# Where the moving tiles of a 256-token transformer kernel lie relative to its weight tiles, modulo 512 bytes

## The reference

```
for layer in range(2):                            # first block, N = 256 tokens
    h = h + mixer(rmsnorm(h, g))                  # x @ w_in, ..., @ w_out
    a, b = split(rmsnorm(h, g2) @ w_in)           # 1024 -> 2 x 3072
    h = h + (gelu(causal_dwconv(a)) * b) @ w_out  # 3072 -> 1024
for l in range(2):                                # second block: 512 tokens (x and context), then 256
    branches, gates = split_in(modulate(rmsnorm(x)) @ w_in[l])
    x = x + g1 * (sum(sigmoid(gate) * (branch @ w_branch)) @ w_out[l])
    x = x + g2 * swiglu(modulate(rmsnorm(x)), w_ffn_in[l], w_ffn_out[l])
return rmsnorm(x, final_g)
```

## Time and profile before

| | us |
|---|---|
| median of 3 runs | 2056.38 |
| lowest and highest run | 2051.12, 2064.75 |
| the profiled execution's own time | 2058.86 |
| its span in the trace | 2057.1 |
| TensorE busy | 1981.9 (96%) |
| VectorE busy | 1498.4 (73%) |
| ScalarE busy | 897.0 (44%) |
| GpSimd busy | 361.3 (18%) |
| TensorE instructions | 12926 matmuls, as many weight loads |

### The profile page before, as it was taken

The page is one execution under the profiler, slowest core; times in us unless marked ns, Lnnn a source line. Parts: engine busy times, 40 slices in busy tenths (PEclk is TensorE's granted clock), DMA queues, the critical chain, the costliest instruction groups (busy, mean ns, idle before and its releaser), DMA issues.

```text
span 2057.1 us, 33908 instructions
## 1 busy us (share of the span) xinstructions
PE 1981.9 (96%) x12926; PEld 1751.6 (85%) x12926; DVE 1498.4 (73%) x2820; ACT 897.0 (44%) x1436; POOL 361.3 (18%) x354
## 2 busy tenths in 40 slices
PE   6999999989999999989999999999999998998998
PEld 6999999859999988646888878888888866998998
DVE  7769987687987698776687667575666986675554
ACT  5744444473445532575343332222224356654443
POOL 0013233002325400001100312202231000013223
PEclk9999999899999999999999999999999999999999
DMA  6455575505555432103345325454563311554552
GB/s 261 164 195 194 190 262 180 198 11 216 201 183 210 166 110 82 42 1 116 131 183 179 117 83 205 143 202 166 204 216 142 141 45 43 184 188 161 188 201 83
DMA packets 46991, 318.15 MB, mean 155 GB/s; under 512 B 5008, under 2 KB 8080, under 8 KB 9488
## 3 DMA queue, kind: packets, MB, share of 16 engines
q1 hardware_dynamic: 45568, 309.60, 41.8%
q0 software_dynamic: 1296, 6.82, 1.0%
HBM read 315.34 MB, written 1.05 MB: 154 GB/s over the span
## 4 chain that ended last, share of the span: by engine, by line
PE 88%; DVE 5%; ACT 4%; issue 1%; POOL 1%; DMA 0%; DVEq 0%; POOLq 0%; ACTq 0%
PE ps L674 85%; ACT arena L1249 3%; PE ps L959 2%; DVE arena L2092 2%; DVE w_lo L1664 1%; ACT w_hi L1249 1%; DVE small L1896 0%; POOL arena L574 0%; DVE arena L1918 0%; PE ps L1152 0%; DMA x<-x_in 0%; POOL arena L570 0%; DVE arena L1646 0%; ACT L1249 0%; PE ps L1145 0%
## 5 line engine op out<-in xcount | busy, mean ns | idle before, releaser
L674 PE MATMUL ps<-h_hi,w_hi 128*128 128x256 f32 (+2 forms) x2656 | 841.0, 317 | 18.0 <-DVE h_lo L1656 6.3
L674 PE MATMUL ps<-h_lo,w_hi 128*128 128x256 f32 (+2 forms) x2656 | 833.4, 314 | 0.0
L674 PE MATMUL ps<-h_hi,w_lo 128*128 128x256 f32 (+2 forms) x2656 | 833.0, 314 | 0.0
L1664 DVE TENSOR_TENSOR w_lo<-ring,w_hi 128x1024 fp32r<-128x1024 f32 x457 | 584.8, 1286 | 291.9 <-ACT w_hi L1249 291.1
L1249 ACT ACTIVATE w_hi<-ring 128x1024 fp32r<-128x1024 f32 x457 | 479.7, 1056 | 516.6 <-PE ps L674 482.8
L674 PEld LDWEIGHTS ps<-h_hi,w_hi 128*128 128x128 f32 (+1 forms) x2656 | 504.4, 190 | 55.6 <-issue 12.2
L674 PEld LDWEIGHTS ps<-h_lo,w_hi 128*128 128x128 f32 (+1 forms) x2656 | 503.3, 189 | 32.3
L674 PEld LDWEIGHTS ps<-h_hi,w_lo 128*128 128x128 f32 (+1 forms) x2656 | 502.7, 189 | 32.4
L1249 ACT ACTIVATE arena<-ps 128x512 f32<-128x512 f32 (+2 forms) x246 | 141.2, 580 | 341.3 <-PE ps L674 297.0
L674 PE MATMUL ps<-hid_hi,w_lo 128*128 128x256 f32 (+1 forms) x736 | 224.0, 304 | 0.0
L674 PE MATMUL ps<-hid_hi,w_hi 128*128 128x256 f32 (+1 forms) x736 | 224.0, 304 | 0.0
(11 more groups left out here) (195 smaller groups left out, 1945.3 us busy)
## 6 DMA issues: line engine op xcount, KB each, us to landing
ring<-wstream SPq DMA_DIRECT2D x290, 1024.0 KB, 4.8
arena<-c_in POOLq DMA_DIRECT2D x7, 512.0 KB, 4.0
arena<-rpb POOLq DMA_DIRECT2D x2, 1536.0 KB, 7.0
x<-x_in SPq DMA_DIRECT2D x2, 1024.0 KB, 12.3
out<-arena SPq DMA_DIRECT2D x8, 128.0 KB, 2.0
cst<-consts SPq DMA_DIRECT2D x1, 940.0 KB, 12.2
prm<-params SPq DMA_DIRECT2D x1, 580.0 KB, 10.9
ring<-wstream SPq DMA_DIRECT2D x1, 512.0 KB, 3.9
```

The lines of the kernel that those rows point to most:

```text
L674: ins = nc.tensor.matmul(*a, **k)
L1664: V.tensor_tensor(w_lo[:, job % SPLITS, :], raw_job(job), w_hi[:, job % SPLITS, :].bitcast(F32), ALU.subtract).then_inc(weights_ready, 1)
```

## The change

It changes the byte offsets of operands and nothing else. The view `h_at[S]` starts 32 floats in, where it started 48 in. The spacer is 16 floats shorter, which moves the arena, and hid_hi and hid_lo behind it, down by 64 bytes. The padding below branch_hi is 16 floats longer, so branch_hi keeps its address, and its view for 256 columns starts 32 floats in. The view of hid_hi and hid_lo for 512 columns starts 32 floats in, where it started 16 in, so it keeps its address as well.

```diff
--- before.py
+++ after.py
@@ -313,7 +313,7 @@
         w_lo = sb("w_lo", [P, SPLITS, JOB * P], F32R)
         x = sb("x", [P, KD, S2])
         h_rows = [sb(n, [P, KD * S2 + 128], F32R) for n in ("h_hi", "h_lo")]
-        h_at = {n: [v[:, at:at + KD * S2].rearrange("p (k t) -> p k t", t=S2) for v in h_rows] for n, at in ((S, 48), (S2, 0))}
+        h_at = {n: [v[:, at:at + KD * S2].rearrange("p (k t) -> p k t", t=S2) for v in h_rows] for n, at in ((S, 32), (S2, 0))}
         prm = sb("prm", [P, PARAM["end"]])
         cst = sb("cst", [P, CONST["end"]])
         ones = sb("ones", [P, P])
@@ -324,7 +324,7 @@
         mod_parts = sb("mod_parts", [P, 48, 2, 2])
         gn = sb("gn", [P, 2, 2, KD])
 
-        sb("spacer", [P, 128 - KD - HEADS])
+        sb("spacer", [P, 112 - KD - HEADS])
         with nc.sbuf_tensor("arena", [P, ARENA], F32) as arena:
             pass
         with ExitStack() as over:
@@ -336,9 +336,9 @@
             cy_lo = place("cy_lo", KC * S2)
             place("below_naq", 4096, F32)
             naq_lo, gq_lo = place("naq_lo", KC * S2), place("gq_lo", KC * S2)
-            place("below_hi", 17104 - 15616, F32)
-            hi_rows = place("branch_hi", 48 + KC * S2)
-        branch_hi = {n: hi_rows[:, at:at + KC * S2].rearrange("p (c t) -> p c t", t=S2) for n, at in ((S, 48), (S2, 0))}
+            place("below_hi", 17120 - 15616, F32)
+            hi_rows = place("branch_hi", 32 + KC * S2)
+        branch_hi = {n: hi_rows[:, at:at + KC * S2].rearrange("p (c t) -> p c t", t=S2) for n, at in ((S, 32), (S2, 0))}
         branch_lo = [v[:].rearrange("p (c t) -> p c t", t=S2) for v in (naq_lo, gq_lo, cy_lo)]
         hid_hi = sb("hid_hi", [P, KF1 * S + 128], F32R)
         hid_lo = sb("hid_lo", [P, KF1 * S + 128], F32R)
@@ -369,7 +369,7 @@
         m_silu, m_prod = (part(hidden_end + i * 2 * S2, 2, S2) for i in range(2))
         f_out = part(0, KD, S)
         f_hidden = [v[:, 0:KF1 * S].rearrange("p (c t) -> p c t", t=S) for v in (hid_hi, hid_lo)]
-        m_hidden = {n: [v[:, at:at + KF1 * S].rearrange("p (c t) -> p c t", t=S2) for v in (hid_hi, hid_lo)] for n, at in ((S, 0), (S2, 16))}
+        m_hidden = {n: [v[:, at:at + KF1 * S].rearrange("p (c t) -> p c t", t=S2) for v in (hid_hi, hid_lo)] for n, at in ((S, 0), (S2, 32))}
 
         n_q = part(0, KD, S)
         n_kc = part(2048, 2, KV, S)
```

## The result

| | before | after |
|---|---|---|
| median, us | 2057.82 | 2082.81 |
| lowest and highest of 6 runs, us | 2051.12, 2066.25 | 2081.76, 2086.03 |
| ratio, with 95% interval | | 1.0121 (1.0095 to 1.0147) |
| span of the profiled execution, us | 2057.1 | 2083.9 |

The forecast was 2049 us in a range of 2036 to 2066; the time lies outside, on the side of rival (d). The page of the kernel after has the same shape as the earlier trace rows: TensorE busy for 96%, the clock at 90% or more in every slice, L674 with 85% of the chain. TensorE's busy time grew by 27.9 us (1981.9 to 2009.8) and the span by 26.8, so what was lost is TensorE's own time; VectorE's busy time stayed (1498.4 to 1498.2).

A forecast was written before the change was run, and what follows sets the result against it. TensorE was taken as the bound: its instruction count times their pace. The profiled 2058.9 us less 9.7 for the quick pace everywhere, small terms at 0, gave 2049.2, said as 2049 us; range 2036 to 2066.

The forecast's parts named there:

- rival (d): 256-column matmuls moved to 128: always the middle pace, 22.6 us more, 2081 us; chance 0.06.
- the count of slow matmuls: 256-column products in the kernel before: 2211 matmuls said to run at a slow pace, taking 258.4 us.
- the seven stretches: Parts of the kernel before at the slow pace, 258.4 us; the quick pace there would save 9.7 us.
- The upper bound of the unknown pace: 256-column matmuls at 128: at most the 120.0 ns seen at 0, which would cost 39.5 us more.
- the reading of the scatter: Runs of the kernel before: may differ by which stages are slow; one feed-forward layer changing pace is 6.6 us.
- a single pace at 128: 256-column matmuls after the change: one pace only, so the after runs would lie close together.
- I take the quick pace, 113.3: 256-column matmuls at 128: 113.3 ns chosen within the bounds, 9.7 us less than the profiled execution.
- reached 113.3 in 7 of 10 matmuls: 256-column matmuls at 192, the nearest row to 128: mostly 113.3 ns, used as ground for 113.3 at 128.
- (c): 256-column matmuls: pace repeats every 128 bytes, so 128 is like 0, 120.0 ns each, 2098 us; chance 0.12.
- (b): 256-column matmuls at 128: conflict vanishes wholly, only the weight load is left, 2036.7 us or 2035; chance 0.08.
- floor of 111.6 ns: Weight load in every matmul, read from matmuls with 60 moving columns; 12.5 us below the quick pace over 7344 matmuls.
- (a): 256-column matmuls at 128: same two paces as 192, 113.3 and 117.7 ns, 2056 us (2050 to 2063); chance 0.16.

The follow-up runs named there:

- bare loop: Kernel before without the reference's computation, TensorE alone running product triples at many operand offsets: 113.3 ns at 192, 120.0 at 0, 118.8 at 128 behind plain matmuls.

## Why the prediction was wrong

**Right.** TensorE's pace at L674 is what sets the time and what the change changes; nothing else in the program moved. The paces, the addresses (0 modulo 256 for the 120.0, 192 for the two of before), and the count of slow matmuls are borne out: the sum over the quick pace, 11.6 us in the kernel before, has the 9.7 us of the seven stretches in it. The upper bound of the unknown pace was right: 118.7 and 120.0 lie in 113.3 to 120.0. So was the reading of the scatter. That the after runs lie close together came true by luck: the reason given was a single pace at 128, and 128 has two, both slow and close to each other.

**Where hid and the arena lie.** No trace holds an address. The sizes ahead of the arena add up to 164 modulo 512; the 192 rested on the author's assumption that eps takes 32 bytes in the place of 4. The paces of hid's tiles bear the 192 out, modulo 256. In the kernel before hid has 113.3 in the first feed-forward part and 117.7 in the second (576 matmuls in 67.6 us). With the arena and hid 64 bytes lower it has 118.7 (550 in 65 us), with hid's view 64 bytes higher 120.0 (502 in 60 us), and with it 176 higher 113.3 (558 in 63 us). Among the 32 offsets in steps of 8 bytes only 192 has these paces at 0, -64, +64 and +176 bytes from it; 160 and 168, which lie around 164, have 117.3 to 120.0 themselves and 118.3 and 120.0 at +176. hid begins 76800 bytes, a multiple of 512, behind the arena, so the arena lies at 192 as well. This row of the kernel before is from the first feed-forward part's second product:

```profile
256.00:319.00 63.00, 63.00 (x559) 63.00 (x558) 51.26 (x87) 30.09 (x33) 20.78 (x16) 1.00 0.70 253
```

**The step that failed** is the choice inside the bounds: "I take the quick pace, 113.3", because 128 is farthest from 0 and 256. It took two points of a map, 0 and 192, and a slope between them that doesn't exist: 192 is 6.7 ns and more from 184 and from 200. What the runs showed at 128 is 118.7 ns, and 120.0 in some stretches, from first to last. With 118.7 as the term, the same sum gives (7344 - 2211) x 5.4 + 2211 x 1.0 = 27.7 + 2.2 = 29.9 us more in the place of 9.7 us less. In the traces the steps over 113.33 ns grew by 41.2 - 11.6 = 29.6 us; the rest of the span was 2.8 us shorter, which no run explains, and the medians are 25.0 us apart.

**The argument that misled beside it**: 192 "reached 113.3 in 7 of 10 matmuls" was taken as speaking for its neighbour. It spoke for 192 alone. Nearness in bytes says nothing here: 0 is twice as far from 128 as 192 is, and its 120.0 was the better guide. Of the 32 offsets in steps of 8 bytes, 13 have 120.0 from both entries and only three (16, 112, 192) showed 113.3 at all.

**The rivals.** (d) gave 2081 us and is the nearest in time, by another pace: not the 117.7 that 192 has when slow but 128's own 118.7, with 120.0 in some stretches. (c), the repeat after 128 bytes, gave 2098; the repeat isn't there, but its reason, that 0 was the only other offset known and slow, was the better guide. (b) didn't come at any offset tried: its floor of 111.6 ns is that of a different stream, plain float32 with 60 moving columns, and 113.3 stays even where 16 weight columns are loaded. That the 111.6 is the weight load fits what the runs show. The mean record of a load grows from 94 ns (16 columns) to 189 (128) in the program with narrow tiles, 0.85 ns a column, which gives 108 for 128 as an estimate. And in the trace of before the moving columns don't set it: with 2 of them behind 128 weight columns the distance is the same, (1.03 - 0.25) / 7 = 111 ns (the last one's own 0.25 us goes off).

```profile
L556 PEld LDWEIGHTS ps<-h_lo,w_hi 128*128 128x128 f32 x1920 | 363.0, 189 | 0.3
...
L556 PEld LDWEIGHTS ps<-h_lo,w_hi 128*16 128x16 f32 x96 | 9.0, 94 | 2.1
...
808.96 1.03 PE L1152 MATMUL ps<-cst,arena 128*128 128x2 f32 x8
```

(a), with a chance of 0.16, was that 128 has the same two paces as 192, 113.3 and 117.7: 2056 us (2050 to 2063), from which the upper end of the range came. It is right in form (128 has 118.7 and 120.0) and wrong in level. Nor is a wait on another engine needed for the loss: in the bare loop no other engine works, and the distance of TensorE's own two operands sets the pace, 113.3 to 120.0 for the four distances tried with shifted weights.

**The chances.** 0.17 was given to slower by over 1%, and 0.55 to one value of a quantity that no row showed. Two known points, 113.3 or 117.7 and 120.0, gave no more ground for the quick end than for the slow one.

## What to carry to other kernels

Where TensorE is the bound and operands are float32r, read the starts of the matmuls, not their durations: two stages with the same instructions and different distances between starts point to where the operands lie, or to one of two paces at the same place. Such a pace isn't smooth in the address (113.3 ns at 192, 120.0 and more at 184 and 200) and isn't fixed by it alone (113.3 or 117.8 at 192), so don't reason from one offset to the next; measure a map with the bare loop, from several entries, and take an offset that is quick from all of them (here 112 modulo 256 for 256 columns, 0 for 512). Here that took away the scatter; the median it didn't change by more than the noise. A stage that a change of layout took from 113.3 ns to 118.7 (the kernel after) or to 120.0 (h and hid at 0) got 4.7 or 5.9% longer. In the kernel after TensorE's busy time grew by 27.9 us; no other engine's grew.

## What the runs showed of the hardware

- One form of instruction (128 x 128 weights, 256 moving columns, float32r) ran at steady means of 113.3, 116.7, 117.3, 117.8, 118.3, 118.7, 120.0 and up to 130.0 ns at a granted clock of 1.00, by the distance of the moving tile to the weight tile. Modulo 256 bytes the map nearly repeats (160 has 117.3, 416 has 118.7). The means from 116.7 to 120.0 in this list lie 1/2, 3/5, 2/3, 3/4, 4/5 and 1 times 6.7 ns above 113.3. 512 columns have 226.7 at best, twice 113.3.
- Two paces can last at the same addresses (192: 113.3 or 117.8; 128: 118.7 or 120.0), in the kernel for 1607 matmuls at 117.8. What chooses between them is open: the code before the stretch has a part, but one and the same program took both.
- With 256 moving columns in float32r nothing was quicker than 113.3 ns, with 16 weight columns (at offsets 0, 128 and 192) or with 128.
- What the mechanism is, inside TensorE or the memory, no run here shows. That the mean losses are simple fractions of one step of 6.7 ns, and that the map nearly repeats after 256 bytes, are all there is to go by.
